# The last sublayer makes no input for a next one, and output blocks are stored per token half behind their own affines

## The chip, the cores and the metric

The kernel runs on one core of a Trainium2 chip. The metric is the device time of one execution in microseconds. A profiled execution gives a span, from the first to the last instruction, and a time of its own that is a little longer.

## The reference, cut to what matters

Two post-norm layers on 640 tokens (512 latent ones, 128 of context), each with three sublayers: a half-step feed-forward, a token mixing, a half-step feed-forward. Every sublayer is modulated on its way in and normalised on its way out:

```
u = x * (1 + scale) + shift                    # input of a sublayer
x = layer_norm(ALPHA * x + w * gate * f(u))    # w = 0.5 for feed-forward, 1 for mixing
layer_norm(x) = (x - mean) * rsqrt(var + eps) * g + b
y_p = _ffn_sublayer(y_p, m_ctx, 2, ...)        # the last sublayer; its x is the output y
```

The outputs are the last x of both groups of tokens and the context keys and values of both layers.

## The kernel before, in words

**Data.** X holds the tokens transposed: eight blocks of 128 features (k = 0 to 7, KD = 8) by 640 tokens. The tokens are worked on in two halves of HT = 320. The second half has latent tokens in its first 192 columns and context tokens in its last 128, and these have different modulations, so an operation that uses scale and shift is cut in two pieces there (SEGS).

**Engines.** Each engine has its own program, written out by hand, and they meet through semaphores. In a list of counters `C`, `C["u"].next()` steps the expected count of a semaphore without an instruction; `link(i)` on VectorE makes it wait for its own instruction i; `mark(i, name)` adds to a semaphore behind i.

**Matrix products** run on TensorE in three passes of rounded values: the left and right operands are split in a high part (Uh, w_hi) and a remainder (Ul, w_lo). For the sublayer's input that split is made by VectorE in `split_u` (lines 1158 and 1159: a cast, then a subtraction).

**End of a sublayer** (`last_products`, one for each engine; `down_halves` on TensorE). The down projection of the last group runs for the first token half and then for the second, in four pairs of blocks each. Behind each pair VectorE adds the result to X and to a running sum (`add_pair`, lines 1170 to 1179). When a half is complete:
1. TensorE makes the mean by a matmul with ones (`mean_of`, line 394), VectorE subtracts it (`centre`, line 1192), ScalarE squares (`squares`, line 839), VectorE adds up the squares (line 1200), TensorE makes the variance (line 400), ScalarE takes the root (line 845).
2. VectorE runs `normalise(h)`: the reciprocal of the root (line 1215), then per block a multiplication of X by it (line 1220, two blocks ahead), `split_u(h, k)` and, for the first half, other steps in between: `add_pair` 1 behind block 1 and `add_pair` 2 behind block 2 of the second half's sum; `add_pair` 3 follows behind normalise(0).
3. ScalarE runs `finish(l, s, h)`, per block: it waits for the multiplication (s_xn) and for a free buffer, makes the modulated input u32 of the next sublayer from X (line 857, one or two pieces), waits for its own result (s_u32), and then applies the norm's gain and bias to X in place (line 863, "affine"), which adds one to s_y.

For the second half this work belongs to the following sublayer's `first_up` or `mixing`, beside that one's first products. Behind the very last sublayer there is none: the program's end calls `centre`, `normalise(1)` on VectorE and `squares`, `deviation`, `finish` on ScalarE with nothing beside them. The last sublayer has l = 1, s = 2; `more` in last_products is false there alone.

**Stores.** The queue of SyncE (SP) loads all weight tiles in order (line 304), waits until s_y has all of its 96 counts (48 for each layer: three sublayers, two halves, eight blocks), and then stores the eight blocks of y, 128 rows of 640 numbers each (line 307). The keys and values were stored by ScalarE's queue in the mixing (lines 992 and 993).

Of the kernel before, what the change touches and what calls it, by code (L numbers as in the profile page):

```python
# [10 lines left out]
ACT = mybir.ActivationFunctionType  # L11
# [4 lines left out]
KD = D // P  # L16
DEPTH = 2
LAT, CTX = 512, 128
T = LAT + CTX
HT = T // 2  # L20
# [22 lines left out]
SEGS = (((0, HT, 0),), ((HT, LAT, 0), (LAT, T, 1)))  # L43
# [42 lines left out]
def check_counts(counts):  # L86
    for c in counts:
        assert c.at() == c.first + DEPTH * c.per_layer, (c.sem, c.at(), c.first, c.per_layer)


def build(nc, a):
    ctx = ExitStack()
    with ctx:
        def sb(name, shape, dt=F32):
            return ctx.enter_context(nc.sbuf_tensor(name, shape, dt))

        def sem(name):
            return ctx.enter_context(nc.semaphore(name))


        X = sb("X", [P, KD, T])
# [19 lines left out]
        lnm = sb("lnm", [P, 2, 2, KD])  # L121
# [5 lines left out]
        def at(name, off, shape, dt=F32):  # L127
            size = 4 * int(np.prod(shape[1:]))
            assert off + size <= zone_bytes, (name, off + size)
            return nc.alloc_sbuf_tensor_at(name, shape, dt, offset=z0 + off)  # L130
# [8 lines left out]
        u32 = at("u32", 35840, [P, 4, HT])  # L139
# [88 lines left out]
        s_u32 = sem("modulated")  # L228
        s_u = sem("u_ready")
# [9 lines left out]
        s_y = sem("post_norm_done")  # L239
# [13 lines left out]
        s_out = sem("y_stored")  # L253
# [27 lines left out]
        @block.sync  # L281
        def _(sp):
            for q in range(4):
                n = FIRST_ADA // 4
                sp.dma_start(ada0[:, q * n:(q + 1) * n, :],
                             a["ada"][q * n:(q + 1) * n].rearrange("c p k -> p c k")).then_inc(s_ada0[q], 16)
            for k in range(KD):
                sp.dma_start(X[:, k, :], a["xT"][k]).then_inc(s_x, 16)
            sp.dma_start(cst[:, :, :], a["dft_small"]).then_inc(s_cst, 16)
            sp.dma_start(ident[:, :], a["eye"]).then_inc(s_cst, 16)  # L290
            sp.dma_start(lng[:, :], a["lng"]).then_inc(s_cst, 16)
            sp.dma_start(lnb[:, :], a["lnb"]).then_inc(s_cst, 16)
            for s in range(2):
                sp.dma_start(w_raw[:, s, :, :], a["wstream"][s]).then_inc(s_wload[s], 16)

            for c in range(QTILE):
                for r in range(ROWS):
                    src = a["rpb"][:, ROWS - 1 - r:2 * ROWS - 1 - r, QTILE - 1 - c:QTILE - 1 - c + TW]
                    sp.dma_start(a["gath"][:, c * ROWS + r, :, :], src).then_inc(s_gath, 16)  # L299

            with sp.Fori(1, DEPTH * TILES // 2) as j:
                for s in range(2):
                    sp.wait_ge(s_wsplit, j * 2 + (s - 1))
                    sp.dma_start(w_raw[:, s, :, :], a["wstream"][j * 2 + s]).then_inc(s_wload[s], 16)
            sp.wait_ge(s_y, DEPTH * PER_LAYER["y"])
            for k in range(KD):
                sp.dma_start(a["yT"][k], X[:, k, :]).then_inc(s_out, 16)
            sp.wait_ge(s_out, 16 * KD)


        @block.tensor
# [478 lines left out]
        def _(act):  # L790
            C = make("use full func mods u32 u xc sq added var std xn y att max exp pt ptc o mrg ada kv wraw whi".split())
# [58 lines left out]
            def finish(l, s, h, between=None):  # L850

                for k in range(KD):
                    act.wait_ge(s_xn, C["xn"].next())

                    act.wait_ge(s_u, C["u"].at() + (h * KD + k - 3))
                    for lo, hi, v in SEGS[h]:
                        i = act.activation(u32[:, k % 4, lo - h * HT:hi - h * HT], X[:, k, lo:hi], ACT.Identity,
                                           bias=lnm[:, v, 1, k:k + 1], scale=lnm[:, v, 0, k:k + 1])
                    i.then_inc(s_u32, 1)
                    C["u32"].next()  # L860
                    act.wait_ge(s_u32, C["u32"].at())
                    col = l * (3 * KD) + (s * KD + k)
                    act.activation(X[:, k, h * HT:(h + 1) * HT], X[:, k, h * HT:(h + 1) * HT], ACT.Identity,
                                   bias=lnb[:, col:col + 1], scale=lng[:, col:col + 1]).then_inc(s_y, 1)
                    C["y"].next()
                    for step in (between or {}).get(k, ()):
                        step()
                if h == 1:
                    C["u"].next(2 * KD)
# [192 lines left out]
            for h in range(2):  # L1062
                for k in range(KD):
                    if h * KD + k >= 4:
                        act.wait_ge(s_u, h * KD + k - 3)
                    for lo, hi, v in SEGS[h]:
                        i = act.activation(u32[:, k % 4, lo - h * HT:hi - h * HT], X[:, k, lo:hi],
                                           ACT.Identity, bias=mods[0][:, v, k:k + 1],
                                           scale=mods[0][:, v, KD + k:KD + k + 1])
# [14 lines left out]
        def _(dve):  # L1084
            C = make("use full func h mods u32 u mean sum sq sqsum added std xc xn att kv max sc exp of fill fev pt o mix mrg ada dve whi".split())
# [17 lines left out]
            def link(i):  # L1103

                i.then_inc(s_dve, 1)
                dve.wait_ge(s_dve, C["dve"].next())

            def mark(i, name):
                i.then_inc(C[name].sem, 1)
                C[name].next()  # L1110

            def free(i):
                i.then_inc(s_free, 1)
                use.next()
                use_no[0] += 1
# [39 lines left out]
            def split_u(h, k):  # L1155
                dve.wait_ge(s_u32, C["u32"].next())
                cols = slice(h * HT, (h + 1) * HT)
                link(dve.tensor_copy(Uh[:, k, cols], u32[:, k % 4, :]))
                mark(dve.tensor_tensor(Ul[:, k, cols], u32[:, k % 4, :], Uh[:, k, cols].bitcast(F32),  # L1159
                                       ALU.subtract), "u")  # L1160
# [48 lines left out]
                        add(k - 1)  # L1209
                add(KD - 1)  # L1210

            def normalise(h, between=None):

                dve.wait_ge(s_std, C["std"].next())
                free(dve.reciprocal(std[:, h, :], std[:, h, :]))
                dve.wait_ge(s_free, use.at())

                def normed(k):
                    x = X[:, k, h * HT:(h + 1) * HT]
                    mark(dve.tensor_tensor(x, x, std[:, h, :], ALU.mult), "xn")  # L1220

                ahead = 2
                for k in range(ahead):
                    normed(k)
                for k in range(KD):
                    if k + ahead < KD:
                        normed(k + ahead)
                    split_u(h, k)
                    for step in (between or {}).get(k, ()):
                        step()  # L1230

            def last_products(l, s, next_q, spares, more, places):

                nxt = (s + 1) % 3
                dve.wait_ge(s_free, use.at())
                low_tile()
                for pair in range(KD // 2):
                    add_pair(mods[s], 0, pair)
                    if pair < len(spares):
                        low_tile(spares[pair])  # L1240
                    if pair == 2:
                        finish_mods(mods[nxt], next_q, l * (3 * KD) + s * KD)
                centre(use_no[0] + 1, 0)
                add_pair(mods[s], 1, 0)
                if more:
                    low_tile()
                between = {k: [lambda pair=pair: add_pair(mods[s], 1, pair)] for pair, k in zip((1, 2), places)}
                if more:
                    between[0] = [low_tile]
                normalise(0, between)  # L1250
                add_pair(mods[s], 1, 3)

            def down(m, n_of, count, ada):
# [301 lines left out]
                mixing(l)  # L1555
                ffn(l, 2)
            centre(use_no[0], 1)
            normalise(1)
            check_counts(C.values())


# [3 lines left out]
PER_LAYER = dict(  # L1565
    tile=TILES, use=USES, full=USES - 6, func=112, h=88, mods=3, u32=NORMS, u=NORMS, mean=6, sum=6, sqsum=6,
    added=6 * (KD - 2), var=6, std=6, xc=NORMS, sq=NORMS, xn=NORMS, y=NORMS, att=96, sc=UNITS, max=UNITS, exp=UNITS,
    pt=UNITS, ptc=UNITS, o=UNITS, of=UNITS, fill=2 * PIECES, fev=2 * PIECES, mix=1, mrg=2 * KD, kv=64,
    ada=3 * ADA_SUB, dve=423, wraw=8 * TILES, whi=TILES)
# [123 lines left out]
```

## Time and profile before

| | us |
|---|---|
| median of 3 runs | 2975.05 |
| lowest and highest | 2974.46, 2975.70 |
| the profiled execution | 2975.69 |
| its span | 2973.9 |
| busy: TensorE, VectorE, ScalarE | 2777.2, 1711.2, 766.6 |

How to read the rows of the sections below. PE is TensorE, DVE VectorE, ACT ScalarE, SPq the queue of SyncE, ACTq that of ScalarE; L863 is line 863 of the kernel before. A row of a timeline has the start, the duration until the last end of the merged instructions, the engine, line and operation, output<-input, shapes, how often (x4), and in brackets how long the engine had been idle and who released it. A row of windows has the stretch and its length, then the busy time of PE, PEld (weight load), DVE, ACT and POOL with their instruction counts, the granted TensorE clock (1.00 is full speed, 2.4 GHz; 0.50 is 1.2 GHz), the busy share of the 16 DMA engines and the GB/s that they moved. Where instructions of one engine overlap in a pipeline, the step from start to start is shorter than a duration.

### The profile page before, as it was taken

To read this page: it belongs to the slowest core of one execution; us is meant where nothing else is said; L and a number is where in the kernel's file an instruction comes from. 1 tells how busy PE (TensorE), PEld (TensorE's weight loads), DVE (VectorE), ACT (ScalarE), POOL (GpSimd) and SP (SyncE) were. 2 spreads that over 40 slices of the span, in tenths; PEclk is the share of its full clock that TensorE was granted. 3 is DMA by queue.
4 is the path that set the end of the run, shared out by engine and by line. 5 is a ranking of instruction groups with operands and counts; after the bars stand their busy time and mean duration, and the time that the engine had idled before them with its cause. 6 is when DMAs were issued, how large, how long until landed. Compare 5 with 4: busy or idle time off the path is not lost.

```text
span 2973.9 us, 47454 instructions
## 1 busy us (share of the span) xinstructions
PE 2777.2 (93%) x18760; PEld 2733.3 (92%) x18760; DVE 1711.2 (58%) x3152; ACT 766.6 (26%) x1091; POOL 0.2 (0%) x4
## 2 busy tenths in 40 slices
PE   0599999989999999999999999998999999999994
PEld 0599999989899999999999999998989999999994
DVE  4465555754566685454576555575456668444456
ACT  0211211343322251121252121134332225111124
POOL 0000000000000000000000000000000000000000
PEclk9899999999999999999999999999999999999997
DMA  6233233212133223223313323322213322322320
GB/s 224 79 128 111 102 130 118 79 68 77 54 128 114 99 86 113 99 99 105 117 61 128 113 99 134 114 78 68 77 53 128 114 98 86 113 99 100 112 85 36
DMA packets 76870, 299.34 MB, mean 101 GB/s; under 512 B 24769, under 2 KB 29121, under 8 KB 52673
## 3 DMA queue, kind: packets, MB, share of 16 engines
q1 hardware_dynamic: 50496, 214.31, 20.8%
q10 hardware_dynamic: 26240, 83.20, 8.3%
q8 instruction: 91, 1.49, 0.2%
q14 instruction: 43, 0.34, 0.0%
HBM read 293.80 MB, written 6.82 MB: 101 GB/s over the span
## 4 chain that ended last, share of the span: by engine, by line
PE 89%; DVE 5%; SPq 4%; issue 2%; ACT 1%; DMA 0%; DVEq 0%; ACTq 0%
PE psum L527 11%; PE psum L526 11%; PE psum L524 11%; PE psum L384 6%; PE psum L385 6%; PE psum L382 6%; PE psum L427 3%; PE psum L430 3%; PE psum L431 3%; SPq L299 3%; PE psum L744 3%; PE psum L747 3%; PE psum L746 3%; PE psum L468 2%; PE psum L472 2%
## 5 line engine op out<-in xcount | busy, mean ns | idle before, releaser
L524 PE MATMUL psum<-Uh,w_hi 128*128 128x320 f32 x2304 | 711.9, 309 | 0.0
L526 PE MATMUL psum<-Ul,w_hi 128*128 128x320 f32 x2304 | 711.9, 309 | 0.0
L527 PE MATMUL psum<-Uh,w_lo 128*128 128x320 f32 x2304 | 711.9, 309 | 0.0
L810 ACT ACTIVATE w_hi<-w_raw 128x2048 fp32r<-128x2048 f32 x170 | 325.1, 1912 | 611.4 <-PE psum L382 318.9
L1101 DVE TENSOR_TENSOR w_lo<-w_raw,w_hi 128x2048 fp32r<-128x2048 f32 x170 | 389.5, 2291 | 82.0 <-ACT w_hi L810 76.8
L526 PEld LDWEIGHTS psum<-Ul,w_hi 128*128 128x128 f32 x2304 | 432.5, 188 | 0.0
L527 PEld LDWEIGHTS psum<-Uh,w_lo 128*128 128x128 f32 x2304 | 432.5, 188 | 0.0
L524 PEld LDWEIGHTS psum<-Uh,w_hi 128*128 128x128 f32 x2304 | 432.5, 188 | 0.0
L1284 DVE TENSOR_TENSOR hf<-sg,psum 128x320 f32<-128x320 f32 x176 | 85.7, 487 | 423.6 <-ACT sg L898 421.7
L385 PE MATMUL psum<-Hh,w_lo 128*128 128x320 f32 x1024 | 316.2, 309 | 0.0
L382 PE MATMUL psum<-Hh,w_hi 128*128 128x320 f32 x1024 | 316.2, 309 | 0.0
L384 PE MATMUL psum<-Hl,w_hi 128*128 128x320 f32 x1024 | 316.2, 309 | 0.0
L898 ACT ACTIVATE sg<-psum 128x320 f32<-128x320 f32 x176 | 76.5, 437 | 867.5 <-PE psum L527 639.1
L468 PE MATMUL psum<-Uh,w_hi 128*128 128x320 f32 x384 | 122.2, 318 | 103.8 <-DVE Ul L1159 98.1
L1121 DVE CUSTOM_DVE_ANT_0 junk<-ada_w,csilu 128x1024 bf16<-128x1024 f32 x144 | 176.0, 1222 | 64.6 <-DVEq L1483 48.4
L1267 DVE SCALAR_TENSOR_TENSOR X<-psum,mods,X 128x320 f32 (+2 forms) x192 | 72.6, 434 | 237.0 <-PE psum L385 237.0
L385 PEld LDWEIGHTS psum<-Hh,w_lo 128*128 128x128 f32 x1024 | 192.5, 188 | 0.0
L382 PEld LDWEIGHTS psum<-Hh,w_hi 128*128 128x128 f32 x1024 | 192.5, 188 | 0.0
L384 PEld LDWEIGHTS psum<-Hl,w_hi 128*128 128x128 f32 x1024 | 192.5, 188 | 0.0
L1123 DVE CUSTOM_DVE_ANT_0 junk<-ada_w,csilu 128x1024 bf16<-128x1024 f32 x144 | 176.4, 1225 | 5.0
L468 PEld LDWEIGHTS psum<-Uh,w_hi 128*128 128x128 f32 x384 | 74.2, 193 | 106.5 <-issue 105.0
L744 PE MATMUL psum<-Uh,w_hi 128*128 128x320 f32 x512 | 158.4, 309 | 0.9 <-DVE Ol L1419 0.9
(223 smaller groups left out, 5183.7 us busy)
## 6 DMA issues: line engine op xcount, KB each, us to landing
w_raw<-in_wstream SPq DMA_DIRECT2D x188, 1024.0 KB, 4.9
ada_w<-in_ada ACTq DMA_DIRECT2D x145, 512.0 KB, 3.6
ada<-in_ada SPq DMA_DIRECT2D x4, 2048.0 KB, 19.9
gath<-in_rpb SPq DMA_DIRECT2D x128, 24.0 KB, 2.2
G<-gath ACTq DMA_DIRECT2D x4, 768.0 KB, 4.5
X<-in_xT SPq DMA_DIRECT2D x8, 320.0 KB, 14.2
yT<-X SPq DMA_DIRECT2D x8, 320.0 KB, 3.4
mask<-in_mask ACTq DMA_DIRECT2D x2, 384.0 KB, 5.0
```

Source lines behind the costliest of these rows:

```text
L382: m1 = pe.matmul(out, wh, rh, start=(k == 0), stop=False)
L384: pe.matmul(out, wh, rl, start=False, stop=False)
L385: mm = pe.matmul(out, wl, rh, start=False, stop=(k == nk - 1))
L468: m1 = pe.matmul(out, wh, rh, start=(k == 0), stop=False)
L524: m1 = pe.matmul(out, wh, rh, start=(k == 0), stop=False)
L526: pe.matmul(out, wh, rl, start=False, stop=False)
L527: mm = pe.matmul(out, wl, rh, start=False, stop=(k == KD - 1))
L744: m1 = pe.matmul(out, wh, rh, start=(k == 0), stop=False)
L810: act.activation(hi, w_raw[:, r, :, :], ACT.Copy).then_inc(s_whi, 1)
L1101: dve.tensor_tensor(lo, w_raw[:, r, :, :], hi.bitcast(F32), ALU.subtract).then_inc(s_wsplit, 1)
L1121: link(dve.tensor_tensor_reduce(junk[:, :], ada_w[:, s, :], csilu[:, 0, :], 1.0, 0.0, ALU.mult, ALU.add, acc4[:, 0, s:s + 1]))
L1123: i = dve.tensor_tensor_reduce(junk[:, :], ada_w[:, s, :], csilu[:, 1, :], 1.0, 0.0, ALU.mult, ALU.add, acc4[:, 1, s:s + 1])
```

## The change

- On ScalarE the last sublayer's `finish` leaves out the wait for a free u32 buffer, the modulation (line 857) and the wait for it; the affine waits for s_xn alone. In both halves.
- On VectorE `normalise(0)` and `normalise(1)` of the last sublayer leave out `split_u`.
- SP stores the output in sixteen pieces, first half first: before each it waits for the count that this block's affine gives (81 to 96). A piece is 128 rows of 320 numbers; a row in HBM is 640 numbers long.
- The other lines keep the expected counts consistent.

```diff
@@ sync, after the weight loads
-            sp.wait_ge(s_y, DEPTH * PER_LAYER["y"])
-            for k in range(KD):
-                sp.dma_start(a["yT"][k], X[:, k, :]).then_inc(s_out, 16)
-            sp.wait_ge(s_out, 16 * KD)
+            for h in range(2):
+                for k in range(KD):
+                    cols = slice(h * HT, (h + 1) * HT)
+                    sp.wait_ge(s_y, DEPTH * PER_LAYER["y"] - 2 * KD + (h * KD + k + 1))
+                    sp.dma_start(a["yT"][k][:, cols], X[:, k, cols]).then_inc(s_out, 16)
+            sp.wait_ge(s_out, 16 * 2 * KD)
@@ scalar, finish(l, s, h)
                 for k in range(KD):
                     act.wait_ge(s_xn, C["xn"].next())
-
-                    act.wait_ge(s_u, C["u"].at() + (h * KD + k - 3))
-                    for lo, hi, v in SEGS[h]:
-                        i = act.activation(u32[:, k % 4, lo - h * HT:hi - h * HT], X[:, k, lo:hi], ACT.Identity,
-                                           bias=lnm[:, v, 1, k:k + 1], scale=lnm[:, v, 0, k:k + 1])
-                    i.then_inc(s_u32, 1)
                     C["u32"].next()
-                    act.wait_ge(s_u32, C["u32"].at())
+                    if (l, s) != (DEPTH - 1, 2):
+
+                        act.wait_ge(s_u, C["u"].at() + (h * KD + k - 3))
+                        for lo, hi, v in SEGS[h]:
+                            i = act.activation(u32[:, k % 4, lo - h * HT:hi - h * HT], X[:, k, lo:hi], ACT.Identity,
+                                               bias=lnm[:, v, 1, k:k + 1], scale=lnm[:, v, 0, k:k + 1])
+                        i.then_inc(s_u32, 1)
+                        act.wait_ge(s_u32, C["u32"].at())
                     col = l * (3 * KD) + (s * KD + k)
                     act.activation(X[:, k, h * HT:(h + 1) * HT], X[:, k, h * HT:(h + 1) * HT], ACT.Identity,
                                    bias=lnb[:, col:col + 1], scale=lng[:, col:col + 1]).then_inc(s_y, 1)
@@ vector, normalise
-            def normalise(h, between=None):
+            def normalise(h, between=None, last=False):
...
-                    split_u(h, k)
+                    if last:
+                        C["u"].next()
+                        C["u32"].next()
+                    else:
+                        split_u(h, k)
@@ vector, last_products
-                normalise(0, between)
+                normalise(0, between, not more)
@@ vector, end
             centre(use_no[0], 1)
-            normalise(1)
+            normalise(1, last=True)
+            C["dve"].next(2 * KD)
```

## Rows read from the trace of the kernel before

**Rows 1.** The page: busy time of each engine, with its share of the span.
```profile
PE 2777.2 (93%) x18760; PEld 2733.3 (92%) x18760; DVE 1711.2 (58%) x3152; ACT 766.6 (26%) x1091; POOL 0.2 (0%) x4
```

**Rows 2.** Windows of the tail: busy time, clock, DMA share, GB/s.
```profile
2905.00:2929.00 24.00, 23.95 (x160) 23.37 (x159) 17.05 (x39) 9.84 (x18) 0.00 (x0) 1.00 0.00 1
2929.00:2940.50 11.50, 0.00 (x1) 0.03 (x1) 10.94 (x29) 5.52 (x9) 0.00 (x0) 0.65 0.00 0
...
2952.76:2965.50 12.74, 0.00 (x0) 0.00 (x0) 9.69 (x24) 11.91 (x24) 0.00 (x0) 0.50 0.00 1
2965.50:2973.90 8.40, 0.00 (x0) 0.00 (x0) 0.16 (x1) 0.00 (x0) 0.00 (x0) 0.50 0.81 312
```

**Rows 3.** Timeline of VectorE, first half's normalise and the add_pairs in it.
```profile
2923.89 1.30 DVE L1220 TENSOR_TENSOR X<-X,std 128x320 f32<-128x320 f32 x3
...
2929.91 0.32 DVE L1158 CAST Uh<-u 128x320 fp32r<-128x320 f32 x1
...
2930.68 1.25 DVE L1170 SCALAR_TENSOR_TENSOR X<-psum,mods,X 128x192 f32<-128x192 f32 x4
...
2933.02 0.49 DVE L1220 TENSOR_TENSOR X<-X,std 128x320 f32<-128x320 f32 x1
...
2938.05 1.25 DVE L1170 SCALAR_TENSOR_TENSOR X<-psum,mods,X 128x192 f32<-128x192 f32 x4
```

**Rows 4.** Timeline of TensorE: its last product and the mean of the second half.
```profile
2928.64 0.31 PE L431 MATMUL psum<-Hh,spare_f_lo 128*128 128x320 f32 x1
2940.50 1.41 PE L394 MATMUL psum<-total,ones 128*128 128x320 f32 x2 [11.55 <-DVE total L1179]
```

**Rows 5.** Timeline of the second half: squares, multiplications, modulations, affines (first and last).
```profile
2942.46 1.26 ACT L839 ACTIVATE sq<-X 128x320 f32<-128x320 f32 x3 [5.11 <-DVE X L1192]
...
2952.76 1.30 DVE L1220 TENSOR_TENSOR X<-X,std 128x320 f32<-128x320 f32 x3
2953.28 0.93 ACT L857 ACTIVATE u<-X,lnm 128x192 f32<-128x192 f32 x2 [2.75 <-DVE X L1220]
...
2954.25 0.65 ACT L863 ACTIVATE X<-X,lnb,lng 128x320 f32<-128x320 f32 x1
...
2954.81 0.92 ACT L857 ACTIVATE u<-X,lnm 128x192 f32<-128x192 f32 x2
...
2964.81 0.65 ACT L863 ACTIVATE X<-X,lnb,lng 128x320 f32<-128x320 f32 x1
```

**Rows 6.** Windows: the half microsecond in which the granted clock falls.
```profile
2932.00:2932.50 0.50, 0.00 (x0) 0.00 (x0) 0.47 (x2) 0.00 (x0) 0.00 (x0) 0.93 0.00 0
```

**Rows 7.** The output's stores: SP's timeline, and their line (issue ns, starts, landing).
```profile
2965.49 5.38 SPq L307 DMA_DIRECT2D yT<-X  x8
...
L307 SPq DMA_DIRECT2D yT<-X x8: 353/722/802, 2965.5 to 2970.1; - x8
...
DMA to landing us min/median/max: 2.2/3.4/3.5
```

**Rows 8.** Windows: one microsecond in the middle of the output's stores.
```profile
2968.00:2969.00 1.00, 0.00 (x0) 0.00 (x0) 0.00 (x0) 0.00 (x0) 0.00 (x0) 0.50 1.04 392
```

**Rows 9.** Lines 304 and 299: SP's issues, ns min/median/max, first and last start.
```profile
L304 SPq DMA_DIRECT2D w_raw<-in_wstream x186: 332/333/352, 117.1 to 2876.1; - x186
...
L299 SPq DMA_DIRECT2D gath<-in_rpb x128: 550/600/2878, 30.6 to 116.1; - x128
```

**Rows 10.** Line 1220, all instances: ns min/median/max, first and last start.
```profile
L1220 DVE TENSOR_TENSOR X<-X,std x96: 481/485/494, 575.2 to 2961.1; 128x320 f32<-128x320 f32 x96
```

**Rows 11.** Stores of keys and values: issue, GB/s over 2161 to 2166 (0.125 us each), landings.
```profile
2162.58 0.63 ACTq L993 DMA_DIRECT2D new_v<-V  x1
...
GB/s 0 0 0 0 0 0 0 0 0 0 0 0 0 0 0 0 0 45 270 287 287 205 299 369 271 66 0 0 0 0 0 0 0 0 0 0 0 0 0 0
...
new_k<-kT ACTq DMA_DIRECT2D x1, 128.0 KB, 2.2
...
DMA to landing us min/median/max: 2.0/2.0/3.9
```

## The prediction

> **What bounds the kernel now.** I read the page first. TensorE is busy for 93% of the span [rows 1], but none of its matmuls is touched: the diff changes the last sublayer's two normalisations and the stores behind them. So the question is what bounds the last 50 us. The windows of the tail answer it [rows 2]: up to 2929 TensorE is busy without a gap (23.95 of 24.00 us), and from there on it has nothing but two short reductions. From 2929 to 2940.5 VectorE is busy 10.94 of 11.50 us; from 2952.76 to 2965.5 ScalarE is busy 11.91 of 12.74; from 2965.5 to the end no engine computes and the DMA engines are at 0.81. Three stages, three limits, and the change touches each of them.
>
> **Part A, first token half: eight splits leave VectorE.** The timeline of VectorE [rows 3] shows normalise(0) from 2923.89: multiplications by std (L1220), a cast and a subtraction per block (L1158, L1159: split_u), and two add_pairs between them, then add_pair 3 at 2938.05. TensorE's mean matmul (L394) waits 11.55 us for this. Its last product started at 2928.64 and took 0.31 [rows 4], so pair 3 lay ready from 2928.95 and VectorE came to it 9.1 us late: VectorE alone sets this stretch. The cast of one block starts at 2929.91 and the next step at 2930.68: 0.77 us per split. Eight splits are 8 x 0.77 = 6.2 us. Checked the other way: normalise(0) took 2938.05 - 2923.89 = 14.16 us; eight multiplications at 0.41 (three take 1.30, the last of them 0.48) are 3.3 and two add_pairs at 2.34 (2930.68 to 2933.02) are 4.7, together 8.0, and 14.16 - 8.0 = 6.2. What is late next: add_pair 3 would start at 2931.85, still 2.9 us behind TensorE, and pair 2 was complete a whole pair earlier (2 blocks x 6 x 3 = 36 matmuls at 24.00/160 = 0.15 us [rows 2], 5.4 us), so the whole 6.2 us counts. ScalarE loses eight modulations (L857) here; its affines (L863) then wait for L1220 only, are over by about 2932.6, and the squares need ScalarE some 3.6 us later. **A = 6.2 us.**
>
> **Part B, mean to reciprocal: unchanged, moved forward.** From 2940.50 (mean matmul) to 2952.76 (first multiplication by std) no line is edited [rows 4, 5]: 12.26 us, now from 2934.3 to 2946.56. One thing could shift: the granted clock is 1.00 up to 2929 and 0.50 in all later windows of the tail [rows 2]; 0.93 in the half microsecond from 2932.0 [rows 6] puts the fall, from 2.4 to 1.2 GHz, at about 2932.4, with the engine idle since 2928.95; the mean matmul would come 1.9 us behind that fall, so both reductions still run at the lower level as now (1.41 us). At twice the clock it would take some 0.7 us by an estimate from this row; if the fall came later than the mean, 0.7 us more would be gained. I take 0, with -0.7 kept for the range.
>
> **Part C, second half: ScalarE's affines follow each other.** Now each block costs ScalarE two modulation pieces (192 and 128 columns, 0.92 us together) and, behind their semaphore, one affine: 2953.28, 2954.81 and so on, 1.51 us per block, the last affine from 2964.81 to 2965.46 [rows 5]. Afterwards only the affine is left. No row shows two affines in a row. The nearest one is the step from an affine to the modulation behind it, the same function on about the same tile: 2954.25 to 2954.81, 0.56 us. From below there are the squares, three of which take 1.26 us, 0.42 each [rows 5]; VectorE delivers at 0.41 (2952.76, three in 1.30). From above the affine's whole 0.65. I take 0.56, as it has the same two per-partition operands. The first affine starts where the first modulation does now, 0.52 us behind the first multiplication. So the last affine ends 0.52 + 7 x 0.56 + 0.65 = 5.1 us behind it, instead of 2965.46 - 2952.76 = 12.7. VectorE's cast and subtraction in this half disappear too; they were beside ScalarE's work and end before the stores were issued, so they count nothing of their own.
>
> **Part D, the stores.** Now all eight (320 KB each) wait for the last affine, are issued from 2965.49 in 5.38 us, and the span ends at 2973.90 [rows 7]: 8.4 us behind the last affine. They run at the rate of the DMA engines, about 390 GB/s with the engines at 1.0 [rows 8]. The later issues take 0.8 us each and the first 0.35 [rows 7]: these queued. After the change SP has sixteen stores of 160 KB with a wait before each. Its last weight load was issued at 2876.1 [rows 9], so nothing but these stores is queued behind the waits, and only the end of the program waits for them. The counts are 81 to 96 of the affines' semaphore, in the order of the affines. The eight of the first half are issued between about 2925 and 2933 and read columns that nobody writes any more; they are hidden behind parts A and B, 12 us ahead of the others. Do they slow VectorE beside them? L1220 lies between 481 and 494 ns in all of its 96 instances, loads of weights beside them or not [rows 10]; I take 0. If that cover were gone, eight stores at 0.42 us of transfer would be 3.4 us. Of the second half, each store is issued 0.03 us behind its affine (2965.46 to 2965.49) if SP keeps up. Transfer: the rows in HBM become 1280 bytes long instead of 2560. The nearest stores are new_k and new_v (runs of 512 and 1024 bytes, 128 KB each): 270 to 370 GB/s in the middle of them, landing after 2.2 and 2.0 us [rows 11]; 160 KB at 300 GB/s are 0.55 us, just within the affines' pace. Issue: 0.33 us for a load of 128 rows behind its own wait, 0.62 for new_v right behind new_k, 0.60 with a step of 0.67 ((116.1 - 30.6)/127) for the gather's 128 stores in a row [rows 9, 11]. I take it that SP keeps ScalarE's pace, 0.56; the upper end is 0.70 (the gather's step and a wait), which is 1.0 us more over seven steps. Landing of the last: between 2.0 (new_v) and 3.5 us (the longest yT store, queued); I take 2.1, as nothing is queued. Then 0.35 us to the end: now the last store starts at about 2970.07, lands 3.5 later, 2973.55, and the span ends at 2973.90.
>
> The Trainium skill speaks against halving stores here ("DMA: Bandwidth & Descriptors", Anatomy of one DMA): about 2.0 us fixed per transfer plus bytes over 436 GB/s, so small transfers lose. By it a 160 KB store lands after an estimated 2.4 us and a 320 KB one after 2.75; the shortest of the 320 KB stores here landed after 2.2 [rows 7], so the row is below the page's fit, and by the page the sum would be 0.3 us larger. Its price per transfer matters only if transfers don't overlap, which is the last rival below.
>
> **The sum.** From the first multiplication by std in the second half to the end of the span: now 2973.90 - 2952.76 = 21.14 us. After: 5.1 (last affine) + 0.03 + 2.1 (landing) + 0.35 = 7.6. C and D give 13.5 us, A gives 6.2, together **19.8 us**. The profiled execution took 2975.69 us (its span plus 1.8), so it would be 2955.9, with a span near 2954.1. It is at the top of the three runs (median 2975.05); against the median the forecast is **2955.3 us**, 0.66% less. A difference under 0.2%, about 6 us, is what can't be told from no change.
>
> **Rivals.**
> First, SP's issue becomes the pace of the second half: 0.70 us per store instead of 0.56, and the last one lands after 3.5 us because the short rows drain slower. That is 1.0 + 1.4 = 2.4 us more: 2957.7. For it: the gather's step of 0.67 and new_v's 0.62. Against it: the loads' 0.33 behind a wait, and half the bytes per store.
> Second, part A doesn't reach the mean: something else is late as well in the first half, a count or ScalarE. Then only 13.6 us remain: 2961.5. Against it: VectorE is without idle there (10.94 of 11.50 us) and its multiplications wait for nobody. If the stores of the first half were released only with the second (the change not doing what it says), about 8 x 0.6 = 4.8 us would be lost instead, 2960.1; the counts in the diff speak against it.
> Third, slower: stores that each sit behind a wait don't overlap, one landing before the next is served. The place is the last eight stores, the price eight landings in a row. At 2.2 us it gives 1.2 + 17.6 + 0.35 = 19.2 us instead of 21.1, still a gain of 2.0 + 6.2 (2966.9). It loses from the point where the end is 6 us later than now: (21.14 + 6.2 + 6.0 - 1.55) / 8 = 4.0 us per store. The longest landing of new_v is 3.9 [rows 11] and gives 2980.5, just no difference; half a microsecond beyond that, 4.4, gives 1.55 + 35.2 - 21.14 - 6.2 = 9.4 us more, 2984.5, the time of this rival as a loss. Against it: the eight stores of now lie 3.4 us each from issue to landing and yet all fit in 8.1 us [rows 7], so they overlap.
>
> **How the numbers follow.** Forecast 0.78; SP's pace 0.10; part A lost or stores late 0.05; stores one by one 0.07, of which 0.01 still faster, 0.03 no difference, 0.03 slower. So faster 0.94, same 0.03, slower 0.03. Range: downwards the affines at 0.42 (1.0 us), the clock (0.7) and half the spread of the runs (0.6), of which I keep 2.1; upwards the first rival with the spread, 2.4 + 0.6, and a little towards the second: 2953.2 to 2959.0.
>
> **What would show it.** Right: no L1158, L1159 and L857 (numbers of now) behind 2923.9; the mean matmul idle for some 5.4 us instead of 11.55; the first reciprocal where it is and the second 6.2 us earlier; last affine 5.1 us behind the first multiplication; SP's issues in two groups, the second one stepping at 0.56; a last landing of some 2.1 us. Wrong: SP stepping at 0.7 or more with ScalarE ahead of it, landings that grow from store to store, or a mean matmul that still waits for another than L1179.

## The result, and the profile after

| | before | after |
|---|---|---|
| median, us (6 runs each) | 2975.73 | 2955.97 |
| lowest to highest | 2974.46 to 2976.61 | 2954.08 to 2957.20 |
| span of the profiled execution | 2973.9 | 2953.9 |

The ratio is 0.9934, with a 95% interval of 0.9921 to 0.9947: 19.8 us less. The forecast was 2955.3 against a median of 2975.05, 19.8 us less, and a span near 2954.1.

The windows of the tail of the changed kernel, with the same columns as [rows 2]:

```profile
2929.00:2934.30 5.30, 0.13 (x1) 0.00 (x0) 5.12 (x14) 1.95 (x4) 0.00 (x0) 1.00 0.34 118
2934.30:2946.56 12.26, 2.84 (x4) 1.00 (x4) 8.32 (x16) 4.14 (x9) 0.00 (x0) 0.50 0.01 3
2946.56:2951.70 5.14, 0.00 (x0) 0.00 (x0) 3.40 (x9) 4.46 (x8) 0.00 (x0) 0.50 0.50 174
2951.70:2953.90 2.20, 0.00 (x0) 0.00 (x0) 0.00 (x0) 0.00 (x0) 0.00 (x0) 0.50 0.55 189
```

The stages are the ones of before, each shorter except the second: VectorE's stretch is 5.3 us instead of 11.5, the middle is still 12.26, ScalarE's stretch 5.1 instead of 12.7, the stores' 2.2 instead of 8.4. The stores of the first half now lie in the first line (DMA share 0.34), those of the second in the third and fourth.

The timelines of VectorE (L1223 is the multiplication by std, L1173 an add_pair's first step), TensorE (L396 is the mean), ScalarE (L866 is the affine) and SP, as [rows 3 to 5] and [rows 7] were before:

```profile
2924.07 1.69 DVE L1223 TENSOR_TENSOR X<-X,std 128x320 f32<-128x320 f32 x4
...
2931.98 1.25 DVE L1173 SCALAR_TENSOR_TENSOR X<-psum,mods,X 128x192 f32<-128x192 f32 x4
...
2946.69 3.30 DVE L1223 TENSOR_TENSOR X<-X,std 128x320 f32<-128x320 f32 x8
```

```profile
2934.44 1.40 PE L396 MATMUL psum<-total,ones 128*128 128x320 f32 x2 [5.31 <-DVE total L1182]
2942.47 1.44 PE L402 MATMUL psum<-sqtotal,ones 128*128 128x320 f32 x2 [6.63 <-DVE sqtotal L1203]
```

```profile
2921.25 0.53 ACT L847 ACTIVATE std<-psum,epsc 128x320 f32<-128x320 f32 x1 [3.78 <-PE psum L402]
...
2947.22 4.46 ACT L866 ACTIVATE X<-X,lnb,lng 128x320 f32<-128x320 f32 x8 [2.75 <-DVE X L1223]
```

```profile
2947.90 4.14 SPq L309 DMA_DIRECT2D yT<-X  x8
```

```profile
L309 SPq DMA_DIRECT2D yT<-X x16: 332/332/348, 2925.3 to 2951.7; - x16
...
DMA to landing us min/median/max: 1.8/1.8/1.8
```

No cast and no modulation is left between the multiplications. The last add_pair starts at 2931.98 instead of 2938.05, the mean waits 5.31 us instead of 11.55, the eight affines are one run of 4.46 us, and each store is issued in 0.33 us and lands 1.8 us after its issue.

**A measure without drift.** The profiled executions differ by some microseconds before they reach the edited code: ScalarE's root for the first half of the last sublayer starts at 2921.07 in the kernel before, 2921.25 in the changed one and 2923.06 in one of the experiments, though everything ahead of it is the same. So I compare the stretch from this root's start to the end of the span. It is 2973.90 - 2921.07 = 52.8 us before and 2953.9 - 2921.25 = 32.65 us after: **20.2 us less**. For all kernels:

| kernel | root starts | span | tail | against |
|---|---|---|---|---|
| before | 2921.07 | 2973.9 | 52.8 | |
| e1, stores alone | 2920.71 | 2967.3 | 46.6 | before: -6.2 |
| e2, no input alone | 2920.98 | 2959.9 | 38.9 | before: -13.9 |
| e3, first half of e2 alone | 2921.51 | 2968.1 | 46.6 | before: -6.2 |
| changed | 2921.25 | 2953.9 | 32.65 | before: -20.2 |
| e4, quarter stores | 2921.08 | 2956.8 | 35.7 | changed: +3.1 |
| e5, first half's stores late | 2921.58 | 2957.8 | 36.2 | changed: +3.6 |
| e6, one by one | 2920.53 | 2962.2 | 41.7 | changed: +9.0 |
| e7, busy TensorE | 2921.27 | 2952.6 | 31.3 | changed: -1.3 |
| e8, two affines on VectorE | 2923.06 | 2955.6 | 32.5 | changed: -0.1 |
| e11, e8 with two queues | 2920.42 | 2952.8 | 32.4 | changed: -0.3 |
| e9, pairs first | 2920.04 | 2949.2 | 29.2 | changed: -3.5 |
| e10, pairs first and busy | 2920.27 | 2948.9 | 28.6 | changed: -4.0 |

### The profile page after: what moved, and what is told of

It is laid out like the page before. It is cut to its first block, busy times and chain, and to the rows that moved or that the text cites. A ratio compares the mean times of both kernels' runs of the same rounds, so it can differ in the third digit from the quotient of the medians.

```text
span 2953.9 us, 47391 instructions
## 1 busy us (share of the span) xinstructions
PE 2777.4 (94%) x18760; PEld 2733.5 (93%) x18760; DVE 1698.3 (57%) x3120; ACT 753.8 (26%) x1067; POOL 0.2 (0%) x4
## 4 chain that ended last, share of the span: by engine, by line
PE 89%; DVE 5%; SPq 4%; issue 2%; ACT 1%; DMA 0%; ACTq 0%; DVEq 0%
PE psum L529 11%; PE psum L528 11%; PE psum L526 11%; PE psum L386 6%; PE psum L387 6%; PE psum L384 6%; PE psum L429 3%; PE psum L433 3%; PE psum L432 3%; SPq L299 3%; PE psum L746 3%; PE psum L748 3%; PE psum L749 3%; PE psum L470 2%; PE psum L474 2%; PE psum L475 2%
```

## The experiments: the parts of the change by themselves

**e1_stores_only.** The kernel before with the edit of SP's stores and no other.

```diff
-            sp.wait_ge(s_y, DEPTH * PER_LAYER["y"])
-            for k in range(KD):
-                sp.dma_start(a["yT"][k], X[:, k, :]).then_inc(s_out, 16)
-            sp.wait_ge(s_out, 16 * KD)
+            for h in range(2):
+                for k in range(KD):
+                    cols = slice(h * HT, (h + 1) * HT)
+                    sp.wait_ge(s_y, DEPTH * PER_LAYER["y"] - 2 * KD + (h * KD + k + 1))
+                    sp.dma_start(a["yT"][k][:, cols], X[:, k, cols]).then_inc(s_out, 16)
+            sp.wait_ge(s_out, 16 * 2 * KD)
```

> The kernel before with the store part of the change alone; all modulations and splits of the last sublayer are kept. If the three stages are separate limits, ScalarE keeps its pace of 1.51 us per block to 2965.5, the last store is issued 0.03 us behind the last affine and the span ends 2.2 us later (as in the changed kernel, 2951.71 to 2953.9): span 2967.7, gain 6.2 us, time near 2969.5. If, as the rival has it, stores behind waits do not overlap and each costs more than the pace of 1.51, the end moves to 1.8 us per store from the first affine (2954.9 + 8 x 1.8 = 2969.3): gain 4.6 us. If stores of half rows were slow, their landing would be over 3 us.

Measured: 2969.8 us median of 10 runs against 2975.84, ratio 0.998 (0.997 to 0.9989); span 2967.3, tail 6.2 us shorter. SP's line, with issue times and landing:

```profile
L309 SPq DMA_DIRECT2D yT<-X x16: 332/332/348, 2925.5 to 2965.1; - x16
...
DMA to landing us min/median/max: 1.8/1.8/1.8
```

The last affine of this execution starts at 2964.44 and takes 0.65, the last store is issued at 2965.1 and lands after 1.8 us. So ScalarE stays the pace and the stores are hidden between its steps; the 6.2 us are what they took of the tail. Stores that don't overlap would have left 4.6.

**e2_no_input_only.** The changed kernel with SP's stores as before: the reverse of the diff above.

> The changed kernel with the stores as before (eight of 320 KB, all behind the last affine); the modulations and splits of the last sublayer are left out in both halves. Expected: the mean of the second half 6.1 us earlier, the affines at 0.545 us each, so the last ends 13.8 us earlier, and the stores cost the old 8.4 us behind it: span 2960.1, gain 13.8 us, time near 2962. Together with the stores alone (6.2) this adds up to 20.0 against 20.0 seen in the spans. If part of the gain hung on the two parts together, for instance because stores now run beside the affines, the sum of the two would be short of 19 or over 21.

Measured: 2961.46 us median of 4 runs, ratio 0.9949 (0.9933 to 0.9966); span 2959.9, tail 13.9 us shorter. The mean, the affines and the stores:

```profile
2934.16 1.41 PE L394 MATMUL psum<-total,ones 128*128 128x320 f32 x2 [5.31 <-DVE total L1180]
...
2946.95 4.47 ACT L864 ACTIVATE X<-X,lnb,lng 128x320 f32<-128x320 f32 x8 [2.75 <-DVE X L1221]
...
2951.44 5.38 SPq L307 DMA_DIRECT2D yT<-X  x8
```

The stores run as in [rows 7], 5.38 us of issues from the last affine on. The two parts add up to 6.2 + 13.9 = 20.1 us against 20.2 for both together: they don't need each other and don't disturb each other.

**e3_first_half_only.** Of e2, the first token half alone. The excerpt shows the two lines that decide this, against e2; the other lines keep the expected counts consistent.

```diff
-                    if (l, s) != (DEPTH - 1, 2):
+                    if (l, s, h) != (DEPTH - 1, 2, 0):
...
-            normalise(1, last=True)
+            normalise(1)
```

> Only the first token half of the last sublayer leaves out its modulations and splits; the second half and the stores are as before. Expected by part A: the mean matmul idles 5.3 us instead of 11.55, everything behind it is as before and 6.1 to 6.2 us earlier: span 2967.8, time near 2969.5. Rival (part A is not on the path): gain under 2 us. The granted clock: the engine is idle for about 5.3 us before the mean matmul; if it falls 3.5 us behind the last product as in the kernel before, it is at 0.50 from 2932.4 on; in the changed kernel it fell only at 2934.3.

Measured: 2969.4 us median of 10 runs, ratio 0.9977 (0.9967 to 0.9986); span 2968.1, tail 6.2 us shorter. The mean and the stores:

```profile
2934.69 1.41 PE L394 MATMUL psum<-total,ones 128*128 128x320 f32 x2 [5.31 <-DVE total L1180]
...
2959.69 5.38 SPq L307 DMA_DIRECT2D yT<-X  x8
```

The mean's wait falls from 11.55 to 5.31 us, and the whole of it reaches the end. With e2 this leaves 13.9 - 6.2 = 7.7 us for ScalarE's stretch of the second half.

## The experiments: what limits the stores

**e4_quarter_stores.** Two stores of 80 KB instead of one of 160 behind each affine of the second half.

```diff
-                    cols = slice(h * HT, (h + 1) * HT)
...
+                    for part in range(1 + h):
+                        w = HT // (1 + h)
+                        cols = slice(h * HT + part * w, h * HT + (part + 1) * w)
+                        sp.dma_start(a["yT"][k][:, cols], X[:, k, cols]).then_inc(s_out, 16)
+                        n += 16
+            sp.wait_ge(s_out, n)
```

> The changed kernel with each store of the second half cut in two of 80 KB (rows of 640 bytes), both behind the same affine: SP has to issue two per 0.545 us. The issues last 0.33 us each alone. If SP needs about 0.38 us from issue to issue (0.33 and a step), two take 0.76 and SP becomes the pace: last issue at 2947.9 + 15 x 0.38 = 2953.6, span near 2955.6, 1.7 us more than the changed kernel. If its step is the 0.6 to 0.7 us that the gather and new_v showed, the last issue comes at 2947.9 + 15 x 0.65 = 2957.7 and the span is near 2959.7. If SP were no limit at all, the span is that of the changed kernel within 0.3 us.

Measured in one execution: tail 3.1 us longer, between the two prices expected for SP. Its line (the sixteen stores of the second half start from 2947.7 to 2954.7) and the DMA engines' busy share (in tenths) and GB/s over 2946 to 2965 in 40 slices:

```profile
L312 SPq DMA_DIRECT2D yT<-X x24: 332/430/432, 2925.2 to 2954.7; - x24
```

```profile
DMA  0000055565655555656550000000000000000000
GB/s 0 0 0 0 0 148 187 156 187 158 189 156 187 160 186 159 187 158 186 162 186 7 0 0 0 0 0 0 0 0 0 0 0 0 0 0 0 0 0 0
```

Back to back an issue takes 0.43 us, and the step is 7.0/15 = 0.47. The DMA engines are busy for 5 to 6 tenths of the time and move 150 to 190 GB/s, about half of what they did in [rows 8], so they don't hold it: SP does. Its own pace, 0.47 us, is below the affines' 0.54. In the changed kernel SP has room, but only some 0.07 us per store. The gather's step of 0.67 [rows 9], which the prediction took with a wait as its upper end of 0.70, was no measure for these stores.

**e5_first_half_late.** All sixteen stores wait at least for the first affine of the second half.

```diff
-                    sp.wait_ge(s_y, DEPTH * PER_LAYER["y"] - 2 * KD + (h * KD + k + 1))
+                    sp.wait_ge(s_y, DEPTH * PER_LAYER["y"] - 2 * KD + max(h * KD + k, KD) + 1)
```

> The changed kernel, but the eight stores of the first half are released only by the first affine of the second half, so that their cover is gone. The prediction priced this twice: 3.4 us (their transfer at the engines' rate) and 4.8 us (eight issues at 0.6). Sixteen stores then run from 2947.9 on: at 2.62 MB over 390 GB/s, 6.7 us and about 2 us around it, the span ends near 2956.7 (+2.8); at the 300 GB/s of half rows, 8.7 us, near 2958.7 (+4.8). If the first half's stores cost nothing anywhere, no change.

Measured in one execution: tail 3.6 us longer; the prediction's two prices for a lost cover were 3.4 and 4.8. The line with its landings, and the DMA engines' share and GB/s over 2946 to 2965:

```profile
L309 SPq DMA_DIRECT2D yT<-X x16: 348/450/457, 2948.2 to 2955.5; - x16
...
DMA to landing us min/median/max: 1.8/1.9/1.9
```

```profile
DMA  0000004999999999999999910000000000000000
GB/s 0 0 0 0 0 0 170 337 329 334 324 334 329 324 332 332 329 337 326 337 337 329 345 38 0 0 0 0 0 0 0 0 0 0 0 0 0 0 0 0
```

Sixteen stores in a row go at 160 KB every 7.3/15 = 0.49 us, 330 GB/s without a gap, with the DMA engines busy for nine tenths. Which of the two sets this pace isn't shown: SP issues back to back here, and its step in e4, with half the bytes, was nearly the same (0.47); the landings don't grow from store to store (1.8 to 1.9 us), as they did to 3.4 in [rows 7], where stores of 320 KB queued. The time of the first half's stores is real, and it is gone from the changed kernel because it lies behind parts A and B.

**e6_one_by_one.** SP waits for every landing before the next issue.

```diff
+                    sp.wait_ge(s_out, 16 * (h * KD + k))
                     sp.dma_start(a["yT"][k][:, cols], X[:, k, cols]).then_inc(s_out, 16)
```

> The changed kernel, but SP waits for the landing of every store before it issues the next: the third rival, made real. Each store then costs its landing, 1.8 us, and a wait: the last eight take 8 x 1.85 = 14.8 us from 2947.9, the span ends near 2963.1, 9.2 us more than the changed kernel and still 10.8 us less than the one before. If landing on an empty queue is shorter than 1.8 us because there is nothing beside it, less. The rival's loss needed 4.0 us per store; this shows how far a store is from that.

Measured in one execution: tail 9.0 us longer. SP's waits from 2940 on (us in total, times, longest) show the landings that it now waits for:

```profile
SPq L309 <- DMA yT<-X: 10.1, 7, 1.4
```

Seven waits of at most 1.4 us, each behind an issue of 0.33: one store per 1.84 us. So this is what the third rival costs when it is made true, 1.84 us per store instead of the 4.0 it needed for a loss, and the kernel would still have been 11 us faster than before.

**e8_two_affines_vector and e11_two_queues.** VectorE makes the affines of blocks 6 and 7 of the second half, behind its last multiplication and with a semaphore of its own (the excerpt shows VectorE's part; BY_VECTOR is 6, and ScalarE's `finish` leaves these two blocks out); e11 also issues their two stores from ScalarE's queue.

```diff
             normalise(1, last=True)
+            for k in range(BY_VECTOR, KD):
+                dve.wait_ge(s_xn, C["xn"].at() - (KD - 1 - k))
+                col = (DEPTH * 3 - 1) * KD + k
+                x = X[:, k, HT:T]
+                dve.tensor_scalar(x, x, lng[:, col:col + 1], lnb[:, col:col + 1], ALU.mult, ALU.add).then_inc(s_yd, 1)
```

> The changed kernel, but the affines of blocks 6 and 7 of the second half are made by VectorE, which is idle behind its eight multiplications, with stores behind its own semaphore. Theory (ScalarE's affines are the pace of the second half, SP has room): ScalarE is done 2 x 0.545 us earlier; VectorE ends its eighth multiplication 3.3 us behind the first and two operations of 0.33 to 0.49 us follow, so both end near 4.0 to 4.3 us instead of 5.0: span 0.7 to 1.0 us shorter, near 2953.0. If SP or the DMA engines were the pace, nothing is gained.

> As e8_two_affines_vector, but the stores of blocks 6 and 7 are issued from ScalarE's queue, which has ended its affines. In e8 the last affine ended 4.0 us behind the first multiplication, 1.0 us earlier than in the changed kernel, and yet the last issue came only 0.2 us earlier, with the issues 0.38 and 0.50 us apart at the end. If SP's issuing is what held them, the two queues let both stores go by 4.1 to 4.5 us and the span ends 6.4 to 6.7 us behind the first multiplication (7.2 in the changed kernel, 7.1 in e8). If the rate of the DMA engines holds them (1.31 MB at the 330 GB/s that half rows reached, 4.0 us, from about 2.0 us on), the end stays at 6.9 to 7.1.

e8: 2955.36 us median of 4 runs, ratio 0.993 (0.9914 to 0.9947), and the tail only 0.1 us shorter. The affines did end earlier, four microseconds behind the first multiplication (2948.48) instead of five; SP's last three issues come at 2952.41, 2952.79 and 2953.29:

```profile
2951.71 0.80 DVE L1579 TENSOR_SCALAR X<-X,lng,lnb 128x320 f32<-128x320 f32 x2
...
2952.41 1.33 SPq L314 DMA_DIRECT2D yT<-X  x3
2952.79 0.95 SPq L314 DMA_DIRECT2D yT<-X  x2
2953.29 0.45 SPq L314 DMA_DIRECT2D yT<-X  x1
```

My theory was wrong here: with affines any faster the stores take over at once. e11, in one execution, moves both last stores to a second queue, which issues them at 2949.55 and 2949.95, beside SP. The second fence has the second queue's line with its landings, and the window of one microsecond behind the issues:

```profile
2945.86 3.30 DVE L1234 TENSOR_TENSOR X<-X,std 128x320 f32<-128x320 f32 x8
2946.39 3.38 ACT L874 ACTIVATE X<-X,lnb,lng 128x320 f32<-128x320 f32 x6 [2.75 <-DVE X L1234]
2947.06 3.06 SPq L313 DMA_DIRECT2D yT<-X  x6
2949.08 0.79 DVE L1581 TENSOR_SCALAR X<-X,lng,lnb 128x320 f32<-128x320 f32 x2
2949.55 0.85 ACTq L1091 DMA_DIRECT2D yT<-X  x2
```

```profile
L1091 ACTq DMA_DIRECT2D yT<-X x2: 361/406/452, 2949.6 to 2950.0; - x2
...
DMA to landing us min/median/max: 2.0/2.2/2.5
...
2950.50:2951.50 1.00, 0.00 (x0) 0.00 (x0) 0.00 (x0) 0.00 (x0) 0.00 (x0) 0.50 1.04 359
```

The last issue starts 4.1 us behind the first multiplication instead of 4.8, but the landing takes up to 2.5 us instead of 1.8, and the end is 6.94 us behind the first multiplication (2952.8 - 2945.86), against 7.2 in the changed kernel and 7.1 in e8. That is the time expected if the DMA engines' rate holds them, and not the 6.4 to 6.7 of the other case. The rate itself was higher than the 330 GB/s that I expected: with two queues issuing, the DMA engines moved 359 GB/s at a share of 1.04. The changed kernel's last stretch has three limits within 0.1 us per block: affines 0.54, SP 0.47, transfer 160 KB/359 GB/s = 0.46.

## The experiments: the reductions and their clock

**e7_busy_tensor.** Needless matmuls, never read, in front of the mean and of the variance of the second half.

```diff
+            def keep_clock(u):
+                for n in range(28):
+                    pe.matmul(bank(u, 1, 0, HT), w_hi[:, 0, n % 16, :], Hh[:, n % 6, 0:HT], start=True, stop=True)
...
             un = next_use()
+            keep_clock(un)
             mean_of(un)
+            keep_clock(un)
             variance_of(un)
```

> The changed kernel with 28 needless matmuls (128 rows by 320 columns, results never read) behind the last product and 28 behind the mean of the second half, so that TensorE is idle for about 1 us before the mean and about 2.5 before the variance. Theory: both reductions (1.40 and 1.44 us at a granted clock of 0.50) then run at 1.00 and take 0.70 each, so the end comes 1.4 us earlier: span near 2952.5. Rival: the clock has fallen anyway, or the reductions take as long because they are bound by something else: span as the changed kernel's 2953.9. If the needless matmuls run past the moment at which the sum is ready, the mean comes later and the kernel loses up to 1 us.

Measured: 2954.69 us median of 4 runs, ratio 0.9931 (0.9914 to 0.9947); tail 1.3 us shorter.

```profile
2928.99 4.26 PE L411 MATMUL psum<-Hh,w_hi 128*128 128x320 f32 x28
2934.36 0.81 PE L396 MATMUL psum<-total,ones 128*128 128x320 f32 x2 [1.11 <-DVE total L1188]
2934.76 4.51 PE L411 MATMUL psum<-Hh,w_hi 128*128 128x320 f32 x28
2941.80 0.81 PE L402 MATMUL psum<-sqtotal,ones 128*128 128x320 f32 x2 [2.52 <-DVE sqtotal L1209]
```

Both reductions take 0.81 us instead of 1.40 and 1.44, at a granted clock of 1.00. The gain is shown in the trace of one execution; the difference of the medians to the changed kernel, 1.3 us, is within the spread of both (2.9 and 3.1 us). With the clock at 0.50 (1.2 GHz), the lost time is 0.6 us per reduction, near the 0.7 of the prediction.

**e9_pairs_first and e10_pairs_first_busy.** With the splits gone VectorE has slack ahead of TensorE's last product, and the order of its steps is free to use it.

```diff
+PAIR3 = 3
...
+                for step in (between or {}).get(-1, ()):
+                    step()
...
+                if not more:
+                    first = use_no[0] - 1
+                    add_pair(mods[s], 1, 1, first + 2)
+                    normalise(0, {-1: [lambda: add_pair(mods[s], 1, 2, first + 3)],
+                                  PAIR3: [lambda: add_pair(mods[s], 1, 3, first + 4)]}, True)
+                    return
```

> The changed kernel with the last sublayer's VectorE work in another order: add_pair 1 in the idle time before the first reciprocal, add_pair 2 right behind that reciprocal, add_pair 3 after six of the eight multiplications, the last two multiplications beside the mean matmul. Theory: with the splits gone VectorE is ahead enough for add_pair 3 to start as TensorE ends its last product (2929.1) or just behind it; it takes 2.45 us, so the mean comes at about 2931.7 instead of 2934.44, a gain of 2.7 us. The mean would then start 2.5 us behind the last product, and no trace so far shows the clock to fall before 3 us, so it takes about 0.7 instead of 1.40 us: gain 3.4 us in all, span near 2950.5. Rival: VectorE is not the limit any more in this stretch and something of TensorE is, gain under 0.5 us.

> The order of e9_pairs_first with 28 needless matmuls between the mean and the variance of the second half, whose results are never read. Expected: the gain of the order, 3.4 us, and 0.6 us for the variance at the full clock, so 4.0 us less than the changed kernel: span near 2949.9, time near 2952. If the two gains are the same one (the clock), the sum is under 3.6 us.

e9: 2951.39 us median of 4 runs, ratio to the kernel before 0.9917 (0.9902 to 0.9932); tail 3.5 us shorter than the changed kernel's. VectorE and TensorE:

```profile
2927.96 1.26 DVE L1174 SCALAR_TENSOR_TENSOR X<-psum,mods,X 128x192 f32<-128x192 f32 x4 [0.25 <-PE psum L434]
...
2930.42 0.78 PE L397 MATMUL psum<-total,ones 128*128 128x320 f32 x2 [2.50 <-DVE total L1183]
2937.83 1.43 PE L403 MATMUL psum<-sqtotal,ones 128*128 128x320 f32 x2 [6.63 <-DVE sqtotal L1204]
```

The last add_pair now waits 0.25 us for TensorE, so the stretch is at its floor with this split of the work: last product, one add_pair, mean. The mean is early enough to run at the full clock (0.78 us), the variance is not. Of the 3.5 us, 2.8 are the order: the mean starts 2930.42 - 2920.04 = 10.38 us behind the root instead of 13.19. The other 0.6 are the clock, and they can't be relied on. The expectation said that no trace so far shows the clock to fall before 3 us; the one of e8 shows the fall 2.0 us behind the last product (last section), ahead of where this mean starts. e10 adds the 28 matmuls in front of the variance: 2951.11 us median of 5 runs, 0.9916 (0.9903 to 0.993), tail 4.0 us shorter than the changed kernel's. Its 0.5 us over e9 are seen in the trace, not in the times. Both beat the changed kernel, by 4.6 and 4.9 us in the medians, which were not measured side by side with it, and by 3.5 and 4.0 in the traces.

## Why the prediction was right

**Part A** said 6.2 us from eight splits at 0.77. e3 measured 6.2 by itself, and the wait of the mean fell by 11.55 - 5.31 = 6.24. What came next in line, the last product, lay 2.9 us ahead of the last add_pair by the prediction (2928.95 and 2931.85), and the same 2.9 in the trace (2929.13 and 2931.98). The second rival, a part A that doesn't reach the mean, is out. The stores beside VectorE, taken as 0, cost it nothing that shows: the multiplications (L1223) lie between 479 and 494 ns in all 96 instances, against 481 to 494 before.

**Part B** said 12.26 us unchanged. From the mean to the first multiplication it is 2946.69 - 2934.44 = 12.25. The step on the clock failed, and that the value came out was luck: the prediction let the clock fall at 2932.4, 1.9 us ahead of the mean, because it had fallen there in the kernel before. In the profiled execution of the changed kernel it fell at about 2934.3, 0.1 us ahead of the mean (the window row is in the last section), so a fall a little later would have taken 0.6 us off. e7 and e9 show that other side: a mean at the full clock costs 0.81 and 0.78 us instead of 1.40. The 0.7 us kept for the range was about the right size.

**Part C** said affines 0.56 apart and the last one done after 5.1 us. They were (4.46 - 0.65)/7 = 0.54 apart, and the last ended 2951.68 - 2946.69 = 5.0 us behind the first multiplication. The nearest row, the step from an affine to the next modulation, was the right one to take; the squares' 0.42, the lower end, would have made the stretch 0.9 us too short. e2 and e3 put the stage at 7.7 us, the prediction at 12.7 - 5.1 = 7.6.

**Part D** said SP keeps the pace and the last store lands after 2.1 us. SP's steps were the affines', the landing 1.8, and the end 0.4 us behind that; from the last affine to the end of the span it was 2.2 us against 2.5 forecast. e1 measured this part by itself: 6.2 us against 8.4 - 2.5 = 5.9. The term that was mis-sized is the landing, 0.3 us: half the bytes land sooner than the shortest store of 320 KB, 2.2 [rows 7], and than the smaller new_k and new_v. The Trainium skill's fit ("DMA: Bandwidth & Descriptors", Anatomy of one DMA; about 2.0 us and the bytes over 436 GB/s) would have made it an estimated 2.4 us, 0.6 above the row. The section gives that fit for transfers issued from GpSimd, and these stores are issued from SP; the prediction doesn't say so. From 2.2 and 1.8 us at 320 and 160 KB the slope is about what that fit says, 0.4 us per 160 KB, and the constant here is by an estimate nearer 1.4.

**The cover** of the first half's stores was priced at 3.4 us from the transfer rate and 4.8 from the issues, and e5 measured 3.6, at 0.49 us per store. The first rival, SP as the pace at 0.70, is out, but closer than it looked: SP's own step is 0.47 against 0.54. The third, stores one after another, is 9.0 us when forced (e6). It doesn't happen by itself: in the changed kernel the stores are issued every 0.54 us and land after 1.8, so three or four are under way at a time.

The 0.4 us between the trace (20.2) and the medians (19.8) is less than the drift of the untouched part between executions.

## What to carry to other kernels

The end of a program has no next stage to hide behind, so what is dead or late there costs its full length: read the tail as stages of its own, name the one engine that limits each, and sum over these; here three rows gave 6.2, 7.6 and 5.9 us, within 0.3 us each. Work that makes an input for nobody is the first thing to look for in an unrolled last step, and stores can start with each finished piece as long as a piece is issued and transferred no slower than the engine in front finishes it (0.47 and 0.46 us against 0.54 here; with pieces of half the size, e4, SP became the limit). When such work is taken away, look again at the order: the slack that it leaves in front of another engine's last result was worth 2.8 us more, and 3.5 with the clock as it was in that execution (e9).

## What the runs showed of the hardware

**When the clock falls.** Rows of three executions: the changed kernel, e4 and e8, each with TensorE's last product and the half microsecond in which the granted clock falls.

```profile
2928.82 0.31 PE L433 MATMUL psum<-Hh,spare_f_lo 128*128 128x320 f32 x1
2934.00:2934.50 0.50, 0.06 (x1) 0.09 (x1) 0.29 (x1) 0.00 (x0) 0.00 (x0) 0.83 0.78 279
```

```profile
2928.65 0.31 PE L437 MATMUL psum<-Hh,spare_f_lo 128*128 128x320 f32 x1
2932.50:2933.00 0.50, 0.00 (x0) 0.00 (x0) 0.50 (x2) 0.38 (x1) 0.00 (x0) 0.54 0.69 243
```

```profile
2930.62 0.31 PE L438 MATMUL psum<-Hh,spare_f_lo 128*128 128x320 f32 x1
2932.50:2933.00 0.50, 0.00 (x0) 0.00 (x0) 0.47 (x3) 0.00 (x0) 0.00 (x0) 0.90 0.00 0
```

A mean between 1.00 and 0.50 puts the fall at about 2934.3, 2932.5 and 2932.9. TensorE's last product ended at 2929.1, 2929.0 and 2930.9, so the fall came 5.2, 3.6 and 2.0 us behind it. The same reading of all executions without needless matmuls gives 5.1 to 5.2 us for the changed kernel, e2, e3 and e5, 3.4 to 3.6 for the kernel before, e1, e4, e6, e9 and e11, and 2.0 for e8. In e9 the mean matmul lay in between and didn't keep the clock up:

```profile
2931.00:2932.00 1.00, 0.20 (x1) 0.00 (x0) 0.84 (x3) 1.00 (x3) 0.00 (x0) 0.72 0.00 0
```

The changed kernel, e4, e5, e6, e8 and e11 run the same TensorE and VectorE instructions up to the fall and yet lie in all three groups, so it is the execution that differs here and not the kernel; what in it decides stays open. A forecast should carry both clocks wherever a reduction starts 2 to 5 us behind the last product. What is shown is the price: reductions of 1.40 to 1.44 us at 0.50 and 0.78 to 0.81 at 1.00.

**Short rows.** Stores with rows of 1280 bytes in HBM ran at 330 GB/s from one queue, with the DMA engines busy for nine tenths (e5), and at 359 from two queues, at a share of 1.04 (e11); those with rows of 2560 bytes ran at 390 [rows 8]. A store of 160 KB landed after 1.8 us whether it was alone (e6) or one of a stream at the affines' pace. SP issued a store of 128 rows in 0.33 us when it had waited, and in 0.43 with a step of 0.47 back to back.
